# Six of the early modulation slots as row dots, with the transform's outer columns copied and shifted on ScalarE

## What is computed

```python
def ada_params(cond, w, b):
    m = jax.nn.silu(cond) @ w + b
    return jnp.split(m, 3, axis=-1)        # shift, scale, gate

hl = rmsnorm(x, norm_g[i]) * (1.0 + sc_l[:, None, :]) + sh_l[:, None, :]
hc = rmsnorm(ctx, norm_g[i]) * (1.0 + sc_c) + sh_c

def fourier_mixer(h, w_in, w_out):
    b, l, _ = h.shape
    u, z = jnp.split(h @ w_in, 2, axis=-1)
    ug = u.astype(jnp.float32).reshape(b, l, FNET_GROUPS, FNET_GROUP_DIM)
    y = jnp.fft.fft2(ug, axes=(1, 3), norm='ortho').real
    y = y.reshape(b, l, D_BRANCH).astype(h.dtype)
    return (y * jax.nn.silu(z)) @ w_out
```

## Time and profile before

| | us |
|---|---|
| runs of the kernel | 945.88, 1551.19, 947.40 |
| median of the three | 947.40 |
| profiled execution, its own time | 944.97 |
| span of that execution, first to last instruction | 943.2 |

### The profile page before, as it was taken

One profiled execution on the slowest core, in us unless ns is written; L12 is line 12 of the kernel. 1 busy time (PEld: TensorE's weight loads), 2 busy tenths in 40 slices (PEclk: granted clock), 3 DMA queues, 4 the chain that ended last, 5 costly groups with the idle time before them and its releaser, 6 DMA issues.

```text
span 943.2 us, 13109 instructions
## 1 busy us (share of the span) xinstructions
PE 924.1 (98%) x4835; PEld 801.5 (85%) x4835; DVE 546.9 (58%) x813; ACT 351.0 (37%) x598; POOL 240.2 (25%) x243
## 2 busy tenths in 40 slices
PE   6999999999999999999999999999999999999996
PEld 6999998888888888888888888888888888888886
DVE  6897869999974422367444444435435445468333
ACT  8353343242232322354323334424323333354223
POOL 5259941746563000014100220012100221011001
PEclk9999999999999999999999999999999999999998
DMA  9762324555545212212211122202121121102222
GB/s 365 287 223 90 113 93 153 191 189 179 195 162 223 65 48 67 90 45 90 86 52 42 44 90 67 68 1 89 67 67 44 44 70 63 58 9 90 90 90 89
DMA packets 28747, 98.78 MB, mean 105 GB/s; under 512 B 3688, under 2 KB 5896, under 8 KB 28448
## 3 DMA queue, kind: packets, MB, share of 16 engines
q1 hardware_dynamic: 26688, 91.10, 28.2%
q0 software_dynamic: 1744, 6.84, 1.9%
q10 hardware_dynamic: 272, 0.26, 0.1%
HBM read 96.07 MB, written 2.10 MB: 104 GB/s over the span
## 4 chain that ended last, share of the span: by engine, by line
PE 89%; DVE 3%; DMA 2%; issue 2%; ACT 2%; POOL 1%; SPq 1%; POOLq 0%; DVEq 0%
PE banks L1725 29%; PE banks L1726 29%; PE banks L1727 29%; DMA raw<-stream 1%; DMA gate<-x_rows 1%; DVE hreg L1246 1%; ACT hreg L919 0%; POOL gate L661 0%; DVE wreg L1200 0%; DVE dist L1210 0%; PE banks L1852 0%; POOL gate L701 0%; DVE ring L1128 0%; PE banks L1870 0%; SPq L440 0%
## 5 line engine op out<-in xcount | busy, mean ns | idle before, releaser
L1725 PE MATMUL banks<-hreg,ring 128*128 128x512 f32 (+2 forms) x940 | 332.2, 353 | 1.9 <-DVE ring L1128 0.9
L1726 PE MATMUL banks<-hreg,ring 128*128 128x512 f32 (+2 forms) x940 | 331.3, 352 | 0.0
L1727 PE MATMUL banks<-hreg,ring 128*128 128x512 f32 (+2 forms) x940 | 329.5, 351 | 0.0
L1110 DVE TENSOR_TENSOR ring<-raw,ring 128x512 fp32r<-128x512 f32 x192 | 141.6, 751 | 244.3 <-ACT ring L713 243.0
L713 ACT ACTIVATE ring<-raw 128x512 fp32r<-128x512 f32 x192 | 118.7, 629 | 362.9 <-PE banks L1727 277.9
L1725 PEld LDWEIGHTS banks<-hreg,ring 128*128 128x128 f32 x940 | 177.3, 189 | 27.0 <-issue 3.6
L1727 PEld LDWEIGHTS banks<-hreg,ring 128*128 128x128 f32 x940 | 176.8, 188 | 22.4
L1726 PEld LDWEIGHTS banks<-hreg,ring 128*128 128x128 f32 x940 | 177.4, 189 | 21.1 <-issue 0.2
L628 POOL TENSOR_TENSOR gate<-xreg,gate 128x257 f32<-128x257 f32 (+1 forms) x64 | 69.2, 1111 | 78.4 <-ACT gate L862 62.2
L1142 DVE CUSTOM_DVE_ANT_0 dist<-raw,gate 128x1024 bf16<-128x1024 f32 x64 | 83.7, 1308 | 3.8
L661 POOL TENSOR_TENSOR gate<-gate 128x512 f32<-128x512 f32 x12 | 17.2, 1430 | 250.7 <-ACT gate L943 249.9
(11 more groups left out here) (230 smaller groups left out, 1095.0 us busy)
## 6 DMA issues: line engine op xcount, KB each, us to landing
raw<-stream SPq DMA_DIRECT2D x148, 512.0 KB, 3.3
gate<-stream SPq DMA_DIRECT2D x10, 512.0 KB, 11.2
gate<-x_rows SPq DMA_DIRECT2D x6, 512.0 KB, 6.8
gate<-x_lat POOLq DMA_DIRECT2D x1, 2048.0 KB, 8.8
xreg<-x_lat POOLq DMA_DIRECT2D x1, 2048.0 KB, 10.7
out<-xreg SPq DMA_DIRECT2D x3, 384.0 KB, 2.6
xreg<-stream SPq DMA_DIRECT2D x2, 512.0 KB, 11.1
gate<-cond_in SPq DMA_DIRECT2D x2, 512.0 KB, 10.8
```

The source lines that it names most:

```text
L1110: dve.tensor_tensor(ring[:, n % 2, 1, c], raw[:, buf, c], f32(ring[:, n % 2, 0, c]), ALU.subtract).then_inc(split_done, 1)
L1725: pe.matmul(out, left[0], right[0], start=start, stop=False)
L1726: pe.matmul(out, left[0], right[1], start=False, stop=False)
L1727: return pe.matmul(out, left[1], right[0], start=False, stop=stop)
```

## The change

One slot more of the shift's eight becomes a "D" slot (six instead of five); two instead of three "P" slots stand between the first transforms. The copy of the two outer columns goes from VectorE to ScalarE for k 0 to 5. For k 6 and 7 ScalarE writes the finished shifted column itself, as scale times column plus a base that VectorE prepares (`shift_base`, behind `transform_lo(2)` and the dots after it). The first block of shifts, behind `transform_lo(5)`, now takes k 0 to 5 instead of 0 to 3, and the one at the end only writes hi and lo for k 6 and 7.

```diff
-START = "PPPPPPPPDPPPDDDD"
-DVE_SHIFT = 5
+START = "PPPPPPPPDPPDDDDD"
+DVE_SHIFT = 6
...
+        base0 = sb("base0", [P, KT, 2])
...
+        base_done, end_shift = sem("shift_base_done"), sem("later_shift")
...
                 act.wait_ge(dft_done, k + 1)
                 b = 2 * (k % 3)
                 src = banks[:, 512 * b:512 * b + 1024].rearrange("p (i n) -> p i n", i=2)
+                if k < DVE_SHIFT:
+                    act.activation(dc[:, k, :], src[:, 0, 0:NB + 1:NB], ACT.Copy).then_inc(row_shift, 1)
+                else:
+                    act.wait_ge(base_done, 2)
+                    for v in range(2):
+                        act.activation(shift0[:, k, v:v + 1], src[:, 0, NB * v:NB * v + 1], ACT.Identity,
+                                       scale=fmul[:, k, v:v + 1],
+                                       bias=base0[:, k, v:v + 1]).then_inc(end_shift, 1)
...
                 dve.wait_ge(hf_hi, 2 * k + 2)
...
-                dve.tensor_copy(dc[:, k, :], src[:, 0, 0:NB + 1:NB]).then_inc(row_shift, 1)
...
-            def add_shift(a, b):
-
-                ends = slice(0, HALF + 1, HALF)
-                k = slice(a, b)
-                dve.wait_ge(row_shift, b)
+            def shift_base():
+
+                k = slice(DVE_SHIFT, KT)
+                dve.wait_ge(ada_used, 2 * KT - DVE_SHIFT)
+                add_bias(mod0[:, k, :], pe_columns(7)[:, 0:KT - DVE_SHIFT, :], bias0[:, k],
+                         KT - DVE_SHIFT)
+                for v, tokens in ((0, LAT), (1, CTX)):
+                    dve.tensor_scalar(base0[:, k, v], mod0[:, k, v], float(np.sqrt(tokens)), None,
+                                      ALU.mult).then_inc(base_done, 1)
+
+            def row_shifts():
+
+                k = slice(0, DVE_SHIFT)
+                dve.wait_ge(early_dot, 2 * DVE_SHIFT)
+                add_bias(mod0[:, k, :], row_mod[:, :, :], bias0[:, k], DVE_SHIFT)
+                dve.wait_ge(row_shift, DVE_SHIFT)
                 link(dve.tensor_tensor(shift0[:, k, :], dc[:, k, :], fmul[:, k, :], ALU.mult))
                 for v, tokens in ((0, LAT), (1, CTX)):
                     link(dve.scalar_tensor_tensor(out=shift0[:, k, v], in0=mod0[:, k, v],
                                                   scalar=float(np.sqrt(tokens)), in1=shift0[:, k, v],
                                                   op0=ALU.mult, op1=ALU.add))
+
+            def add_shift(a, b):
+
+                ends = slice(0, HALF + 1, HALF)
+                k = slice(a, b)
                 dve.wait_ge(hf_lo, 2 * b)
...
                 if k < DVE_SHIFT - 1:
-                    early(12 + k)
+                    early(KT + 9 - DVE_SHIFT + k)
                 if k == 4:
                     fold_lo(0)
                 if k == 5:
-                    dve.wait_ge(early_dot, 2 * DVE_SHIFT)
-                    add_bias(mod0[:, 0:DVE_SHIFT, :], row_mod[:, :, :], bias0[:, 0:DVE_SHIFT], DVE_SHIFT)
-                    dve.wait_ge(ada_used, 2 * KT - DVE_SHIFT)
-                    add_bias(mod0[:, DVE_SHIFT:KT, :], pe_columns(7)[:, 0:KT - DVE_SHIFT, :],
-                             bias0[:, DVE_SHIFT:KT], KT - DVE_SHIFT)
-                    add_shift(0, KT // 2)
+                    row_shifts()
+                    add_shift(0, DVE_SHIFT)
+                if k == KT - DVE_SHIFT:
+                    shift_base()
             fold_lo(1)
-            add_shift(KT // 2, KT)
+            dve.wait_ge(end_shift, 2 * (KT - DVE_SHIFT))
+            add_shift(DVE_SHIFT, KT)
```

## The result

The changed kernel takes 947.83 us (median of 20 runs, 946.58 to 949.04), the kernel before 945.54 (median of 20, of which one took 1551.19). The ratio is 1.0022, its 95% interval 1.0015 to 1.0028. That is small against 2%, but well clear of noise. The forecast was 946.2 us, in a range from 944.0 to 949.0, and its sum was +0.14 us over the kernel before. The measured time lies in that range, but the difference is +2.3 us. (The table of the kernel before has a median of 947.40 from three runs; twenty put it at 945.54. Against 947.40 the forecast reads as a gain of 1.2 us, and the loss as 0.4.)

What follows compares the result with a forecast made beforehand. VectorE's chain was taken to set the end, TensorE having slack there. The added pair less removed copies, bias addition and holds put the fourth quarter +0.14 us later; forecast 946.2 us, range 944.0 to 949.0.

Steps and rivals of the forecast that it cites:

- the dot beside GpSimd's fold: First dot of `early(14)` on VectorE: may begin 46.1 to 46.8, still ends 47.9 to 48.0, absorbing earlier delays.
- the tile's 1.76 us: One `ada_tile` of 16 matmul records leaves TensorE; its 1.76 us turn into waits for VectorE.
- one for one: Whatever moves the start of the fourth quarter of `project_u(0)`, 60.93 us before, moves the kernel's end equally.
- five copies of 0.07: Term of VectorE's sum: -0.35 us for column copies leaving VectorE.
- Free of that it is 1.10, to 55.97: VectorE's block at k=5: without the cast's hold beside GpSimd's memsets, 1.10 us instead of 1.84, ending at 55.97.
- The prediction's own sign of being wrong: TensorE's third quarter of `project_u(0)` starting before 58 or after 59.6, or changed spacing after 61; forecast start 58.84.
- I take 0 and keep 0.54 for a rival: Cast at k=5 beside GpSimd's second DMA issue: bounds 0 and 0.54 us, counted as 0.
- Rival 2: Cast in the block at k=5 is held, costing 0.54 us; with +0.14 together +0.7, 946.8 us; chance 0.22.
- Rival 3: VectorE's pair paid in full, cast and fold holds finding other instructions: +1.65 to +2 us, 948.0; chance 0.12.
- Rival 1: VectorE's slip hides, TensorE sets the pace and gains the tile's time: -1.76 us, to 944.4; chance 0.18.
- rival 4: ScalarE's copies lengthen VectorE's waits for its scaling by 0.2 us each; worst case 1.2; no separate chance.
- `fold_lo(0)` beside the memsets: VectorE's `fold_lo(0)` at 52.6 to 53.8 meets GpSimd's memsets: bounds 0 and 0.74 us, taken as 0.

Runs made afterwards that it cites:

- run 9: Changed kernel with both plain-x DMA issues moved from GpSimd to SyncE and GpSimd's fold of slot 2 held until VectorE's second fold: 945.32 us, ratio 0.9999.
- run 1: Changed kernel with GpSimd's two DMA issues held until the first shift and its fold of slot 2 until VectorE's second fold: 945.21 us, ratio 0.9996.
- run 2: Changed kernel with GpSimd's fold of slot 2 ahead of its two DMA issues instead of behind them: 945.78 us, ratio 1.0003.
- run 5: Changed kernel with only GpSimd's fold of slot 2 held until VectorE's second fold, DMA issues left in place: 945.16 us, ratio 1.0001.
- run 12: Changed kernel with only GpSimd's fold of slot 2 held, until the first shift, DMA issues left in place: 945.79 us, ratio 1.0003.
- run 3: Changed kernel with five slots on VectorE as before, keeping the copies and last shifts on ScalarE: 943.65 us, ratio 0.9979.
- run 6: Changed kernel with GpSimd's DMA issues held until the first shift, its fold of slot 2 directly behind them: 945.44 us, ratio 1.0002.
- run 8: Kernel before with GpSimd's DMA issues held until the first shift and its fold of slot 2 until VectorE's second fold: 945.96 us, ratio 1.0004.
- run 4: Kernel before with six slots on VectorE, copies and all shifts staying on VectorE: 948.35 us, ratio 1.0028.

## Why the prediction was wrong

**What bounds the kernel, and the chain on VectorE.** Right. VectorE set the end, the dot beside GpSimd's fold did absorb what lay before it, and the tile's 1.76 us turned into waits. Every duration up to the block at k=5 held within 0.05 us, and run 9 gives the whole sum to 0.04. The end of `project_u(0)` moved by 1.97 us in the profiles and their time by 1.61, so "one for one" held within 0.4. A slip in the bookkeeping changes nothing: of the "five copies of 0.07" only four lie behind 47.96 (49.11, 51.43, 54.59, 55.71), and the sum goes by the listed starts.

**The step that failed** is the block at k=5: "Free of that it is 1.10, to 55.97". It took 2.90 (54.92 to 57.82). Two terms were missing: the bias addition held by 0.72 (0.89 - 0.17) and the cast held by 1.06 (1.24 - 0.18), together 1.78 of the 1.86 by which `fold_lo(1)` came late. The prediction's own sign of being wrong, a third quarter after 59.6, came with them: 60.76. Runs 1 and 9 take both holds away and the time is back at that of the kernel before.
- For the cast, "I take 0 and keep 0.54 for a rival": the trace had the same instruction held for 0.74 beside GpSimd, and the choice went to the other row. The bound was too low as well. It came from the place of the cast as the sum had it, 55.7; one hold ahead of it pushed it to 56.45, right onto the fold at 56.36, and a fold is 1.28 long. The prediction had used `fold_sum(2)` only against `fold_lo(1)`, and had found it over in time.
- The bias addition was not looked at, although it stood in the list of what the block holds. It was read as one of the small instructions, with the row of a quiet time.

**Rivals.** Rival 2 had the place but too small a price (0.54 for 1.78). Rival 3 said it best: the holds "do not vanish but find other instructions", +1.65 to +2, 948.0; measured at the end of the group +1.94, and 947.83 as the median. It had a chance of 0.12. That its time fits to 0.2 us is in part luck: it stood on a base of 946.1, and the kernel before is 945.54. Rival 1 did not come, TensorE waits for VectorE ahead of each of the first three quarters; of rival 4, a copy on ScalarE cost 0.06 us and not 0.2. The cast of before (0.74) and the fold of before (0.77) went, and 0.72 and 1.06 came.

**From the group to the time.** +1.94 at the end of `project_u(0)` stands against +2.3 in the medians. The clock, which no step counted, is the likely rest: 0.85 us in the one of two profiles that shows it. How often it falls was not counted, so this part is argued. That the medians of runs 1, 2, 5 and 12 lie 2.0 to 2.7 below the changed kernel's, where their distances from the first fold explain 1.1 to 1.5, points the same way: each shortens the wait of 2.19 us (to 0.25, 1.16, 0.82 and 0.82). That the weights landed later in more of the changed kernel's executions would do it too, and is not excluded.

**`fold_lo(0)` beside the memsets** was rightly put at nothing: 1.29 us for its two halves at 52.66, 1.28 before, with the memset from 53.25. The rule on two SBUF inputs from the Trainium skill, "SBUF — State Buffer", section "Who interferes with whom", drawn on in the prediction, held there. It did not hold for the bias addition, a `tensor_tensor` too, beside an issue with the fold behind it; there the measurement decides. The last subtraction, expected behind `fold_sum(3)`, came just ahead of it (61.33 against 61.36) and took 0.17; in run 5 it came 0.03 after and took 1.27.

**ScalarE's part** was costed at nothing, and by run 9's sum it is that. Without the sixth slot (run 3) it gains 1.8 us: the VectorE chain is then short enough that TensorE no longer waits in `project_u(0)`. The whole loss is the sixth slot's: 943.65 with five, 947.83 with six, on otherwise the same code. The five-slot form (run 3) beats both kernels.

## What to carry to other kernels

When work is put in front of a chain of short instructions, follow each of them, small ones too, against the other engine's timeline, shifted as well; an instruction of 0.17 us that comes just after a GpSimd fold has started can cost the fold's 1.3 us (1.24 for the cast here). Price such holds as a set, since one moves the next into its own, and check where a removed hold lands (runs 6 and 8). Before more is moved from TensorE, see whether it waits anyway: here 0.7 us off VectorE's chain (16.98 to 16.32) came with a gain of 1.8 us, and 1.76 us off TensorE with none.

## What the runs showed that was not expected

- A bias addition of 128x12 is held until 0.36 us after the second DMA issue starts (55.81 and 55.45), 0.72 us in all, if a fold stands directly behind the issues, and not at all if a wait stands between (three profiles and two).
- TensorE's granted clock fell to 0.50 for some 3 us after a wait of 2.19 us in one execution of the changed kernel and not in another; where it fell it cost 0.85 us. Run 4 kept 1.00 after a wait of 2.37.
- A cast that starts 0.08 us after a memset of GpSimd had 0.17 us (run 3); in the kernel before one that came 0.22 us after took 0.92.
